# Mixture-of-experts blocks: gate and up products by halves, rows turned by VectorE, one store of full rows

## The reference, cut to what matters

```python
scores = sigmoid(t @ w_router);  eidx = top_k(masked(scores + router_bias), 2)
hid = silu(xblk @ w_gate[e]) * (xblk @ w_up[e])     # 1024 -> 512, twice
yblk = hid @ w_down[e]                              # 512 -> 1024
y[token] += yblk[row] * weight[row]                 # two rows per token
```

## Time and profile before

| | |
|---|---|
| Time, 3 runs | 1262.36 us median (1259.98 to 1269.05) |
| Profiled execution | 1263.5 us; its span 1261.4 us |
| Mean granted TensorE clock | 0.977 of full speed |
| PE / PEld busy | 1141.9 us (91%) / 646.6 us (51%) |
| DVE / ACT / POOL busy | 516.3 (41%) / 194.0 (15%) / 248.1 us (20%) |
| DMA | 329.89 MB, mean 262 GB/s |
| Gate and up products, L1449 | 201.3 + 87.8 us busy, 5056 records |
| Down products, L1462 | 108.0 + 46.4 us busy |
| Turning the rows, L1418 | 92.3 us busy, 648 records |

### The profile page before, as it was taken

One profiled execution on the slowest core, in us unless ns is written; L12 is line 12 of the kernel. 1 busy time (PEld: TensorE's weight loads), 2 busy tenths in 40 slices (PEclk: granted clock), 3 DMA queues, 4 the chain that ended last, 5 costly groups with the idle time before them and its releaser, 6 DMA issues.

```text
span 1261.4 us, 27574 instructions
## 1 busy us (share of the span) xinstructions
PE 1141.9 (91%) x10552; PEld 646.6 (51%) x10553; DVE 516.3 (41%) x1426; ACT 194.0 (15%) x475; POOL 248.1 (20%) x307
## 2 busy tenths in 40 slices
PE   3899999999899999999977499999989999999976
PEld 0444444445344566666654244444446666666642
DVE  0245644436246633333323451213484333333327
ACT  1212233334112000000000250111110000000010
POOL 0011100000000323332322350600004333333321
PEclk9899999999898999999999799999989999999988
DMA  8932199996426197899999684333157959999955
GB/s 320 383 131 91 68 323 334 340 355 248 167 35 233 53 392 264 296 365 395 398 399 395 219 280 171 110 120 136 49 218 258 393 185 362 389 397 391 393 209 198
DMA packets 123384, 329.89 MB, mean 262 GB/s; under 512 B 17128, under 2 KB 29840, under 8 KB 123216
## 3 DMA queue, kind: packets, MB, share of 16 engines
q1 hardware_dynamic: 90208, 288.98, 60.7%
q10 hardware_dynamic: 26704, 20.71, 5.6%
q0 software_dynamic: 6432, 19.67, 4.8%
HBM read 312.53 MB, written 25.18 MB: 268 GB/s over the span
## 4 chain that ended last, share of the span: by engine, by line
PE 70%; DVE 9%; DMA 8%; SPq 7%; issue 3%; ACT 2%; POOL 0%; ACTq 0%; POOLq 0%; DVEq 0%
PE PS L1449 17%; PE PS L1462 10%; PE PS L1370 9%; PE PS L1269 8%; PE PS L1527 7%; SPq L337 6%; PE PS L1418 5%; DMA ring<-in_e_down_dram 4%; PE PS L1290 4%; PE PS L1199 3%; PE PS L1301 2%; DVE mx L857 2%; DMA ring<-in_w_ada_dram 2%; DMA UR<-expert_rows,yidx 1%; PE PS L1302 1%
## 5 line engine op out<-in xcount | busy, mean ns | idle before, releaser
L1449 PE MATMUL PS<-ring,RE 128*32 128x256 f32 x3520 | 201.3, 380 | 20.2 <-DMA ring<-in_e_up_dram 10.3
L1449 PEld LDWEIGHTS PS<-ring,RE 128*32 128x32 f32 x3520 | 126.0, 110 | 91.0 <-issue 39.3
L1109 DVE TENSOR_TENSOR RE<-RE,PS 128x64 f32<-128x64 f32 x160 | 32.2, 201 | 285.4 <-ACT RE L686 285.4
L1370 PE MATMUL PS<-ring,UR 128*128 128x512 f32 x256 | 112.9, 595 | 1.9 <-ACT G L646 1.1
L1462 PE MATMUL PS<-ring,RE 128*32 128x256 f32 x1760 | 108.0, 386 | 6.9 <-DMA ring<-in_e_down_dram 6.7
L1527 PE MATMUL PS<-ring,UR 128*128 128x512 f32 x256 | 110.8, 593 | 2.6 <-ACT UR L711 2.6
L686 ACT ACTIVATE RE<-PS 128x128 f32<-128x128 f32 x80 | 22.2, 277 | 532.1 <-PE PS L1449 526.7
L1418 PEld LDWEIGHTS PS<-ident,RE 32*128 32x128 f32 x648 | 83.4, 210 | 35.0 <-issue 32.5
L1269 PE MATMUL PS<-ring,UR 128*128 128x512 f32 x224 | 98.4, 593 | 0.7 <-ACT UR L574 0.7
L1418 PE MATMUL PS<-ident,RE 32*128 32x32 f32 x648 | 92.3, 282 | 0.8 <-DMA RE<-tokens,gidx 0.8
L1449 PE MATMUL PS<-UR,RE 128*32 128x256 f32 x1536 | 87.8, 380 | 3.0 <-DMA UR<-in_e_up_dram 3.0
(11 more groups left out here) (260 smaller groups left out, 1239.9 us busy)
## 6 DMA issues: line engine op xcount, KB each, us to landing
ring<-in_w_ada_dram SPq DMA_DIRECT2D x24, 2048.0 KB, 12.5
ring<-in_e_down_dram SPq DMA_DIRECT2D x22, 2048.0 KB, 24.6
ring<-in_e_gate_dram SPq DMA_DIRECT2D x22, 2048.0 KB, 17.8
ring<-in_e_up_dram SPq DMA_DIRECT2D x22, 2048.0 KB, 18.2
UR<-in_e_up_dram SPq DMA_DIRECT2D x10, 2048.0 KB
RFW<-in_e_down_dram SPq DMA_DIRECT2D x10, 2048.0 KB, 27.0
UR<-in_e_gate_dram SPq DMA_DIRECT2D x10, 2048.0 KB
expert_rows<-RE ACTq DMA_DIRECT2D x320, 32.0 KB
```

Of the source, the lines that this page charges most:

```text
L1370: ins = mm(PS[:, 2 * (j % 2) + half, :], uT[:, k, j * P:(j + 1) * P], w[half][:, k, :], start=(k == 0), stop=(k == DC - 1))
L1449: ins = mm(PS[BLK * q:BLK * q + BLK, 0, 0:2 * P].rearrange("p (g b i) -> p g b i", g=2, b=FC), xT[:, k, :], wgu[:, :, k, :, q, :], start=( ...
```

## The change

The weights of gate and up are loaded with eight neighbouring input rows on each partition, so that a partition takes one run of 16 KB from each matrix instead of four of 4 KB. The gate and up product is made in two halves of the hidden columns, in banks 0 and 1, with 128 moving columns instead of 256 and twice as many products; each half has its own semaphore, silu, multiplication and transpose. A block's rows are gathered as 128 quarter rows of 1 KB, four partition groups of 32, straight to two buffers `xq`; VectorE turns them there in one instruction (`x_turn`), and scales and shifts them out of SBUF, the turn and the scaling between the two halves of the hidden block, the shift behind them. TensorE's transposes, GpSimd's copy and one wait fall away. The result of a block is put together by VectorE in four multiplications, one for each quarter, each on 32 partitions, into 32 full rows; ScalarE stores them with one DMA. ScalarE's loop is turned around, so that the store of a block stands ahead of the silus of the next. TensorE reads the next block range in the middle of the down product. The order of the rows' indices is made for quarter rows (32 small products instead of 8), and the folded scale is laid out as the weights are.

```diff
-        xg = RE[0:BLK, 0:1024]
-        xga = [RE[0:BLK, 2688:3712], RW[0:BLK, 1024:2048]]
+        xq = [RE[:, 2176 + 256 * b:2432 + 256 * b] for b in range(2)]
+        xs = RE[:, 0:256].rearrange("p (c s) -> p c s", c=DC)
         xT = RE[:, 1024:1280].rearrange("p (c s) -> p c s", c=DC)
         xTt = RE[:, 1280:1536].rearrange("p (c s) -> p c s", c=DC)
         gs = RE[:, 1536:1664]
         hid = RE[:, 1664:1792]
         hidT = RE[:, 2048:2176]
-        ysb = [RE[:, 2176 + 256 * b:2432 + 256 * b] for b in range(2)]
+        ysb = [RE[0:BLK, 2688:3712], RW[0:BLK, 1024:2048]]
         ohlo = RW[:, 2048:2304].rearrange("p (n s) -> p n s", s=BLK)
         ohhi = RW[:, 2304:2304 + 8 * NCOL].rearrange("p (n b) -> p n b", b=NCOL)
 
...
                 b = moe_place[l][par][j][0]
                 dst = slots[b]
                 if j < 2:
-                    src = (e_gate, e_up)[j][l, e].rearrange("(k p r) n -> p k (r n)", p=P, r=2)
-                    dst = dst.rearrange("p (k n) -> p k n", k=DC // 2)
+                    src = (e_gate, e_up)[j][l, e].rearrange("(p k) n -> p k n", k=DC)
+                    dst = dst.rearrange("p (k n) -> p k n", k=DC)
                 else:
                     src = e_down[l, e].rearrange("(k p) n -> p k n", p=P)
                     dst = dst.rearrange("p (k n) -> p k n", k=FC)
...
                 for j in range(NT):
                     pool.wait_ge(s_hw[j], 16 * l + 16)
 
-                def gather(rows, done, col):
+                def gather(b, col):
                     nc.gpsimd.indirect_dma_start(
-                        out=rows, out_offset=None, in_=hscr[l],
-                        in_offset=bass.IndirectOffsetOnAxis(ap=col, axis=0)).then_inc(done, 16)
+                        out=xq[b], out_offset=None, in_=hscr[l].rearrange("t (q n) -> (t q) n", q=CG),
+                        in_offset=bass.IndirectOffsetOnAxis(ap=col, axis=0)).then_inc(xg_in[l][b], 16)
 
                 pool.wait_ge(ix_rd, l + 1)
-                gather(xg, x0_in, gidx[:, 0:1])
-                gather(xga[1], xg_in[l][1], gidx[:, 1:2])
-                gather(xga[0], xg_in[l][0], gidx[:, 2:3])
+                for b in range(2):
+                    gather(b, gidx[:, b:b + 1])
                 pool.wait_ge(tab_rd, l + 1)
                 pairs = pool.value_load(table[l][0:1, NE + 1:NE + 2], min_val=1, max_val=MAXB // 2)
                 with pool.Fori(0, pairs) as gg:
                     for par in range(2):
                         g = gg * 2 + par
-                        pool.wait_ge(xg_in[l][1 - par], gg * 16 + 16)
+                        pool.wait_ge(xs_rd[l], g + 1)
                         pool.nop(nofuse=True)
-                        nc.gpsimd.tensor_copy(gcol[:, 1 - par:2 - par], gidx[:, bass.ds(g + 3, 1)]).then_inc(gc_used[l], 1)
-                        pool.wait_ge(xt_pe[l], g + 1)
-                        pool.nop(nofuse=True)
-                        nc.gpsimd.tensor_copy(xg, xga[1 - par]).then_inc(xg_rd[l], 1)
+                        nc.gpsimd.tensor_copy(gcol[:, par:par + 1], gidx[:, bass.ds(g + 2, 1)]).then_inc(gc_used[l], 1)
                         pool.wait_ge(gc_used[l], g + 1)
                         pool.nop(nofuse=True)
-                        pool.wait_ge(xg_rd[l], g + 1)
-                        pool.nop(nofuse=True)
-                        gather(xga[1 - par], xg_in[l][1 - par], gcol[:, 1 - par:2 - par])
...
                 A(G[:, 0:256], PS[:, 4, 0:256], ACT.Copy).then_inc(gb_ev, 1)
                 act.wait_ge(tab_rd, l + 1)
-                pairs = act.value_load(table[l][0:1, NE + 1:NE + 2], min_val=1, max_val=MAXB // 2)
+                pairs = act.value_load(table[l][0:1, NE + 1:NE + 2], min_val=NE // 2, max_val=MAXB // 2)
                 A(warm[:, :], ones[:, 0:1], ACT.Silu)
-                with act.Fori(0, pairs) as gg:
+
+                def silu(h, g):
+                    act.wait_ge((gu_a, gu)[h][l], g + 1)
+                    A(gs[:, 64 * h:64 * h + 64], PS[:, h, 0:64], ACT.Silu).then_inc(silu_rd[l], 1)
+
+                def store(par, g):
+                    act.wait_ge(y_ev[l], g + 1)
+                    act.nop(nofuse=True)
+                    act.dma_start(yscr[l][bass.ds(g * BLK, BLK), :], ysb[par]).then_inc(y_st[l][par], 16)
+
+                for h in range(2):
+                    silu(h, 0)
+                with act.Fori(0, pairs - 1) as gg:
                     for par in range(2):
                         g = gg * 2 + par
-                        act.wait_ge(gu[l], g + 1)
-                        A(gs, PS[:, 0, 0:P], ACT.Silu).then_inc(silu_rd[l], 1)
-                        act.wait_ge(y_ev[l], g + 1)
-                        act.nop(nofuse=True)
-                        for q in range(CG):
-                            act.dma_start(yscr[l][bass.ds(g * BLK, BLK), 256 * q:256 * q + 256],
-                                          ysb[par][BLK * q:BLK * q + BLK, :]).then_inc(y_st[l][par], 16)
+                        store(par, g)
+                        for h in range(2):
+                            silu(h, g + 1)
+                g = act.value_load(table[l][0:1, NE + 3:NE + 4], min_val=NE - 2, max_val=MAXB - 2)
+                store(0, g)
+                for h in range(2):
+                    silu(h, g + 1)
+                store(1, g + 1)
                 rows_loaded(l == 0)
                 if l == DEPTH - 1:
                     for j in range(1, NT):
...
-                V_.tensor_copy(gidx[:, :], PS[0:BLK, 6, 0:NCOL]).then_inc(ix_rd, 1)
+                V_.tensor_scalar(gidx[:, :], PS[:, 6, 0:NCOL], piece[:, 0:1], None, ALU.add).then_inc(ix_rd, 1)
 
                 loop = dlp[l]
 
-                def x_evac(lnk):
-                    lnk(V_.tensor_tensor(xTt, PS[:, 2, 0:DC * BLK].rearrange("p (c s) -> p c s", c=DC),
-                                         fold_p[:, 0, l, :].unsqueeze(2).broadcast_to([P, DC, BLK]), ALU.mult))
+                def x_turn(b):
+                    V_.transpose(xs, xq[b].rearrange("p (d c) -> p c d", c=DC)).then_inc(xs_rd[l], 1)
+
+                def x_scale():
+                    return V_.tensor_tensor(xTt, xs, fold_p[:, 0, l, :].unsqueeze(2).broadcast_to([P, DC, BLK]), ALU.mult)
+
+                def x_shift():
                     V_.tensor_tensor(xT, xTt, fold_p[:, 1, l, :].unsqueeze(2).broadcast_to([P, DC, BLK]),
                                      ALU.add).then_inc(xT_rd[l], 1)
 
                 affine(l, NT - 2)
-                dve.wait_ge(xt_pe[l], 1)
+                dve.wait_ge(xg_in[l][0], 16)
+                x_turn(0)
+                dve.wait_ge(xs_rd[l], 1)
                 dve.wait_ge(fold_in, 16)
-                x_evac(link)
+                link(x_scale())
+                x_shift()
                 affine(l, NT - 1)
                 dve.wait_ge(gb_ev, 2 * l + 2)
                 pairs = dve.value_load(table[l][0:1, NE + 1:NE + 2], min_val=1, max_val=MAXB // 2)
                 with dve.Fori(0, pairs) as gg:
-                    k = [0]
-
-                    def lnk(ins):
-                        k[0] += 1
-                        ins.then_inc(loop, 1)
-                        dve.wait_ge(loop, gg * 6 + k[0])
-
                     for par in range(2):
                         g = gg * 2 + par
-                        dve.wait_ge(silu_rd[l], g + 1)
                         for h in range(2):
                             cut = slice(64 * h, 64 * h + 64)
-                            lnk(V_.tensor_tensor(hid[:, cut], gs[:, cut], PS[:, 0, P + 64 * h:P + 64 * h + 64], ALU.mult))
+                            dve.wait_ge(silu_rd[l], gg * 4 + (2 * par + h + 1))
+                            V_.tensor_tensor(hid[:, cut], gs[:, cut], PS[:, h, 64:128], ALU.mult).then_inc(loop, 1)
+                            dve.wait_ge(loop, gg * 6 + (3 * par + 2 * h + 1))
                             V_.transpose(hidT[:, cut], hid[:, cut]).then_inc(ht_rd[l][h], 1)
-                        dve.wait_ge(xt_pe[l], g + 2)
-                        x_evac(lnk)
-                        dve.wait_ge(y_st[l][par], gg * 16 * CG + 16 * CG)
+                            if h == 0:
+                                dve.wait_ge(xg_in[l][1 - par], gg * 16 + 16 * par + 16)
+                                x_turn(1 - par)
+                                dve.wait_ge(xs_rd[l], g + 2)
+                                x_scale().then_inc(loop, 1)
+                        x_shift()
+                        dve.wait_ge(y_st[l][par], gg * 16 + 16)
                         dve.wait_ge(dn_pe[l], g + 1)
-                        V_.tensor_tensor(ysb[par], PS[:, 5, 0:256], G[:, 0:256], ALU.mult).then_inc(y_ev[l], 1)
-                    assert k[0] == 6
+                        for q in range(CG):
+                            quarter = slice(BLK * q, BLK * q + BLK)
+                            ins = V_.tensor_tensor(ysb[par][:, 256 * q:256 * q + 256], PS[quarter, 5, 0:256], G[quarter, 0:256],
```

(45 more changed lines are left out.)

23 lines of the change are left out of this document (13 added, 10 removed).

## The result

The changed kernel takes 1225.07 us (median of 4 runs, 1224.35 to 1228.28) beside 1264.79 before (4 runs): ratio 0.9688, 95% interval 0.9659 to 0.9717. The profiled execution has a span of 1223.4 us (before 1261.4).

| us | layer 0: before, after | layer 1: before, after |
|---|---|---|
| first gather issued | 420.9, 424.1 | 946.5, 930.4 |
| gather to first product | 6.3, 5.0 | 6.2, 4.8 |
| to the fourth follow-up load | 84.0, 77.0 | 76.1, 70.6 |
| to the last landing | 180.8, 169.7 | 184.4, 171.5 |
| to the first result gather issued | 17.4, 17.3 | 14.6, 12.5 |

What follows compares the result with a forecast made beforehand. TensorE's block period was taken to bound each layer's first stretch, full DMA engines the second. Savings 14.5 + 1.6 + 9.2 + 2 + 2.4 = 29.7 us from 1263.5 gave 1233.8, as a median 1233 us; range 1216 to 1264.

Steps and rivals of the forecast that it cites:

- second stretches: Per layer, from the fourth follow-up expert load to the last landing: ten experts' loads, 181 us, set by DMA bytes.
- The two stretches: Each layer's expert phase: TensorE's block period sets the first, DMA the second; faster blocks shorten only the first.
- Gate and up by halves at no cost: TensorE's gate and up: 128 narrow records at 27 ns each take 3.5 us, as long as before.
- rival (f): Gate and up on TensorE: narrow products keep 54 ns, period 9.3 us, 1446 us total; chance 3%.
- rival (g): Small loss of another kind, from clock or loop code twice as long: 1275 to 1285 us; chance 4%.
- The new loop, 5.8 us: Round through VectorE, ScalarE and TensorE sets a 5.8 us block period instead of 6.43; 14.5 us saved over 23 distances.
- Start of the loop: Landing, turn, scale and shift take 1.5 us instead of 3.2, about half hidden: 2 x 0.8 = 1.6 us saved.
- Gather: Quarter-row gather lands 10.5 us after the turn, within 11 us allowed; just fits, no cover to spare, priced at nothing.
- rival (e): Gathers land late behind large weight packets, period 9.1 us while weights stream, 1327 us total; chance 13%.
- DMA rate: Second stretch: 16 KB packets speed the 20 gate and up matrices by 4%, 4.6 us per layer.
- the small gap: Second stretch: the gap after the fifth follow-up load, 1 us saved per layer.
- Tail: Behind the last landing: shorter down, gate and up and wait, longer result, three store issues fewer; 2 x 1.2 us saved.

Runs made afterwards that it cites:

- e6: Changed kernel with ScalarE's order turned: first-half silu of the next block, then the store, then second-half silu; 1222.08 us, ratio 0.9658.
- e2: Kernel before with only the gate and up products cut into two halves of 128-column products in two banks, one signal, one silu; 1269.51 us, ratio 1.0028.
- e4: Changed kernel with gate and up not halved: 32 products of 256 columns into one bank, one signal, one silu; 1284.0 us, ratio 1.0135.
- e7: Changed kernel with VectorE's turn of the gathered rows doubled, one more 128x256 turn per block into a scratch tile; 1266.53 us, ratio 1.0001.
- e9: Changed kernel with ScalarE's wait for the fold vectors' stores and their load moved behind the second tile of layer 0's norm and routing; 1224.24 us, ratio 0.9662.
- e3: Changed kernel with gate and up weights loaded by two DMAs each, no packet over 4 KB; 1235.86 us, ratio 0.9758.
- e1: Kernel before with only gate and up weights in 16 KB runs, product order and fold vectors laid out to match; 1260.78 us, ratio 0.9958.
- e5: Changed kernel with the result part undone: one multiplication of 128 partitions and four stores of 32 KB per block; 1246.08 us, ratio 0.9839.
- e10: Changed kernel with one result multiplication and four stores, both silus of the next block ahead of the stores; 1228.46 us, ratio 0.9684.
- e8: Changed kernel with e_down also in 16 KB runs and gate and up columns read with a stride of four; 1500.68 us, ratio 1.1854.

## Why the prediction was right, and where its terms were off

It said 1233 in 1216 to 1264, faster; measured 1225. Of the 38.2 us that the stages bring, the second stretches have 24.0 (11.2 said), the first ones 12.4 (14.5), the starts of the loop 2.8 (1.6) and the tails 2.2 (2.4); the later start of layer 0 takes 3.2 off. The places of the gain were foreseen, the largest of them at less than half its size, and two smaller errors went the other way. Its steps:

- **The two stretches.** Right: everything saved lies in them and at their ends, and e6's 0.3 us per block changed only the first.
- **Gate and up by halves at no cost.** Right in the stream (3.67 us with 128 records, 3.70 in e2), so rival (f) falls. The 27 ns of the prediction are not what its row gives: (0.64 - 0.27) / 16 is 23. The rule of the Trainium skill ("TensorE: Matmul & The Clock Gate", Back-to-back issue gap), 81 ns each, is not borne out here: the records have 29. The small cost of longer code that rival (g) named is likely real: distances of 8.2 and 8.0 us in the first pass. Its other half, the clock, cost nothing that shows.
- **The new loop, 5.8 us.** Right, 5.71 and 5.77 in turn, by errors that cancel: the four multiplications, each on another group of 32 partitions, run one behind another, 0.43 apart (1.71, not 1.47), without the overlap that was counted; why is not shown. The rest was 0.3 shorter. The turn took 0.61 (0.6 said), the scaling 0.42. e4, e6 and e7 show that the chain through result, store, silu and turn is what counts, and e4 that the halves carry it: without them the change would have lost. First stretches: 7.0 and 5.5 us less (7.6 and 6.9 said). The first pass ate what it should have gained (the first five distances of layer 0 took 33.2 us, before 33.5), and the eight-block expert of layer 0 gained more than said: its blocks were 6.62 to 6.66 us apart before, where the prediction took 6.43 from a block behind the first stretch.
- **Start of the loop.** 1.3 and 1.4 us gained (0.8 said). Unforeseen: layer 0 starts 3.2 us later. ScalarE's wait for the fold vectors had no margin left in the kernel before; e9 takes it off.
- **Gather.** It fits, with more cover than said; rival (e) did not come. In the window 560 to 660 us the first packet of a gather came 4.2 us after issue (before 4.1), though 16 KB packets stood ahead, the last had ended at 5.8, and it had landed at 7.1 (medians of 14 gathers; 9.4 was said). A gather of quarter rows shows as 32 packets of 4 KB, just like one of full rows, so two per engine on average and not the eight that were counted. The earlier trace rows shows equal shares of two queues; it does not show that they alternate packet by packet. And "price nothing" missed a gain.
- **DMA rate: the mis-sized term.** 4.6 + 1 us per layer said, 11.1 and 12.9 measured. The 4% for the packets was right in size: e3 puts it at 4 us per layer. The other 7 to 9 us come without large packets, and the sum had only the 1 us of the small gap for them. e3 shows two parts of them: less engine time for gathers and stores (9.7% instead of 12.1) and slightly quicker weight packets. And e1 shows that beside the old gathers large packets bring no higher rate, and at most 1.4 us per layer up to the last landing. The sum had no term for the gathers' and stores' packets, neither for their own time nor for what they do to the packets beside them. How the second part divides between the gather's form and GpSimd's copy stays open.
- **The single store.** I counted it as three issues fewer. It is worth more: without it and VectorE's assembly the kernel takes 21 us longer (e5), 0.5 us of the 0.7 per block by a later signal behind the down products whose cause is open, and beside 16 KB weight packets some of the small store pieces land too late (e1, e10).
- **Tail.** 0.1 and 2.1 us (1.2 said for each).

## What to carry to other kernels

When a loop runs beside a full DMA queue, look at all its packet sizes together: here large weight packets alone brought no rate (e1), and paid beside quarter-row gathers into all partitions and larger stores (e3 against the changed kernel). Small stores beside them need buffers for a longer landing (e1, e10). Moving work off TensorE onto VectorE helps only if the result of the first half starts the chain early; work out the round through all engines, then look which issue in it can stand behind the next signal (e6). A wait that ends just in time is a cost of the next change.

## What the runs showed of the hardware

- Reading the moving operand with a stride of four fp32 doubled a stream of 128-column products, 3.67 to 7.57 us (e8).
- Away from gathers a 16 KB weight packet took 612 to 614 ns and a 4 KB one 160 to 163. While a gather's packets ran, a 16 KB packet took 732 with gathers into 32 partitions and GpSimd's copy (e1), and 627 with gathers into 128 and no copy (changed kernel).
- Two stores of 1 KB pieces beside 16 KB packets landed 9.8 and 11.5 us after issue and held up the chain (e10, e1). The last packet of a block's stores came 6.4 us after the last issue in the median of layer 0 (e1); in the changed kernel, with 32 rows of 4 KB, 4.9.
- An extra instruction of 0.60 us in the chain of engines cost 1.06 us per block (e7).
- The four multiplications on groups of 32 partitions took 1.71 us, 0.43 each, as long as one on 128 partitions (0.42 in e5).
